# The setup stage of a two-layer diffusion trunk: tiles of x moved ahead of the first modulation's weights

## What is computed

```
silu_c, silu_cc = jax.nn.silu(c), jax.nn.silu(c_ctx)
for l in range(DEPTH):
    mods  = jnp.split((silu_c  @ mod_w[l] + mod_b[l])[:, None, :], 6, axis=-1)
    cmods = jnp.split((silu_cc @ mod_w[l] + mod_b[l])[None, None, :], 6, axis=-1)
    zl = modulate(rmsnorm(xl, norm1_g[l]), mods[0], mods[1])
    zc = modulate(rmsnorm(xc, norm1_g[l]), cmods[0], cmods[1])
    ...
```

## Time and profile before

| | us |
|---|---|
| median of 3 runs (3260.53 to 3262.33) | 3261.51 |
| the profiled execution's own time | 3260.64 |
| its span, first to last instruction | 3258.2 |
| PE busy in the span | 3042.1 (93%) |
| DVE busy | 1581.9 (49%) |
| ACT busy | 1077.6 (33%) |
| mean granted TensorE clock | 0.974 |

### The profile page before, as it was taken

The page is one execution under the profiler, slowest core; times in us unless marked ns, Lnnn a source line. Parts: engine busy times, 40 slices in busy tenths (PEclk is TensorE's granted clock), DMA queues, the critical chain, the costliest instruction groups (busy, mean ns, idle before and its releaser), DMA issues. The chain is left out here.

```text
span 3258.2 us, 40429 instructions
## 1 busy us (share of the span) xinstructions
PE 3042.1 (93%) x17039; PEld 2500.8 (77%) x17039; DVE 1581.9 (49%) x1953; ACT 1077.6 (33%) x1241; POOL 348.5 (11%) x365
## 2 busy tenths in 40 slices
PE   3799895899999999999989999999989999999997
PEld 2577674787888888888877888888867878888886
DVE  3567565336444544444556333333335455445545
ACT  2477575223111111211235434433323222222122
POOL 0011111510000000000023222222110000000002
PEclk8899998999999999999999999999998999999998
DMA  6233331612212211122111111111041111111111
GB/s 255 68 108 106 111 90 35 240 47 91 65 59 65 65 57 54 59 65 65 59 38 39 38 38 39 41 41 40 11 143 46 46 46 46 52 52 46 46 46 52
DMA packets 217451, 220.50 MB, mean 68 GB/s; under 512 B 34366, under 2 KB 191645, under 8 KB 211131
## 3 DMA queue, kind: packets, MB, share of 16 engines
q1 hardware_dynamic: 206443, 161.38, 16.2%
q0 software_dynamic: 10480, 56.52, 5.2%
q10 hardware_dynamic: 352, 0.06, 0.0%
HBM read 191.58 MB, written 26.34 MB: 67 GB/s over the span
## 5 line engine op out<-in xcount | busy, mean ns | idle before, releaser
L741 PE MATMUL ps<-zH,wH 128*128 128x512 f32 (+1 forms) x2160 | 582.3, 369 | 17.4 <-DVE zL L619 11.0
L741 PE MATMUL ps<-zH,wL 128*128 128x512 f32 (+1 forms) x2160 | 578.2, 368 | 0.0
L741 PE MATMUL ps<-zL,wH 128*128 128x512 f32 (+1 forms) x2160 | 578.0, 367 | 0.0
L741 PEld LDWEIGHTS ps<-zH,wH 128*128 128x128 f32 x2160 | 373.7, 188 | 109.0 <-issue 30.3
L741 PEld LDWEIGHTS ps<-zL,wH 128*128 128x128 f32 x2160 | 373.4, 188 | 70.3
L741 PEld LDWEIGHTS ps<-zH,wL 128*128 128x128 f32 x2160 | 373.4, 188 | 70.3
L1824 DVE SCALAR_TENSOR_TENSOR res<-ps,mod,res 128x1024 f32<-128x1024 f32 x240 | 236.7, 1014 | 189.7 <-PE ps L741 178.3
L751 DVE SCALAR_TENSOR_TENSOR V<-ps,vec,V 128x1023 f32<-128x1023 f32 (+1 forms) x132 | 134.1, 1016 | 391.6 <-ACT V L1697 388.5
L1673 ACT ACTIVATE wH<-wraw 128x1024 fp32r<-128x1024 f32 x130 | 134.5, 1050 | 391.9 <-PE ps L741 391.9
L741 PE MATMUL ps<-hH,wH 128*128 128x512 f32 (+1 forms) x700 | 193.2, 373 | 0.0
L741 PE MATMUL ps<-hL,wH 128*128 128x512 f32 (+1 forms) x700 | 191.1, 370 | 0.0
(11 more groups left out here) (276 smaller groups left out, 4627.8 us busy)
## 6 DMA issues: line engine op xcount, KB each, us to landing
wraw<-in_ffn_w_up_dram SPq DMA_DIRECT2D x88, 512.0 KB, 3.8
modw<-in_mod_w_dram POOLq DMA_DIRECT2D x40, 1024.0 KB, 5.3
wraw<-in_ffn_w_down_dram SPq DMA_DIRECT2D x44, 512.0 KB, 3.6
wraw<-in_na_w_in_dram SPq DMA_DIRECT2D x24, 512.0 KB, 4.8
modring<-in_mod_w_dram SPq DMA_DIRECT2D x8, 1024.0 KB, 8.2
wraw<-in_rg_w_in_dram SPq DMA_DIRECT2D x16, 512.0 KB, 6.3
bias<-scratch_bias SPq DMA_DIRECT2D x32, 224.0 KB, 4.2
scratch_yT<-GG POOLq DMA_DIRECT2D x10, 640.0 KB, 3.3
```

The costliest lines, as they stand in the source:

```text
L741: last = nc.tensor.matmul(ps[:, slot * SLOT + c:slot * SLOT + c + n], w(k), r(k)[:, c:c + n], start=(k == 0 and i == 0), stop=(k == K - 1 ...
```

## The change

SP loads x and ctx ahead of all eight blocks of modulation weights; blocks 4 to 7 keep their waits and now follow blocks 0 to 3 directly. PE transposes all eight columns of x directly after the small vectors and runs the eight modulation steps one after the other behind them. A wait of PE for `vec_ready` is dropped; `c_ready`, which it still waits for, comes after it on ACT. The stores of x on SP stand where they stood, behind block 7. ACT's, DVE's and POOL's lists are as before.

```diff
@@ SP @@
             for tile, row, k, s in vec_dmas:
                 sp.dma_start(m.vraw[row:row + k, tile, :], s).then_inc(vec_in, 16)
-            for q in range(4):
-                mod_weights(sp, q)
             for i in range(NT):
                 s = t["x"][0, i * P:(i + 1) * P, :] if i < SEQ // P else t["ctx"][0, i * P - SEQ:(i + 1) * P - SEQ, :]
                 sp.dma_start(m.xraw[:, i, :], s).then_inc(x_in[i], 16)
-            for q in range(4, KD):
-
-                sp.wait_ge(mod_used, q - 3)
+            for q in range(KD):
+                if q >= 4:
+                    sp.wait_ge(mod_used, q - 3)
                 mod_weights(sp, q)
             for f in range(KD):
@@ PE @@
             ins.then_inc(vec_T, 1)
-            pe.wait_ge(c_ready, 2)
-            pe.wait_ge(vec_ready, 2)
-            pe.wait_ge(mod_clear, 1)
-            for k in range(4):
-                modulation(k)
             for f in range(KD):
                 s = f % 2
                 if f >= 2:
@@
                     ins = nc.tensor.transpose(ps[:, s * SLOT + i * P:s * SLOT + i * P + P], m.xraw[:, i, f * P:(f + 1) * P], m.ident[:, :])
                 ins.then_inc(xT_done, 1)
-            for k in range(4, KD):
+            pe.wait_ge(c_ready, 2)
+            pe.wait_ge(mod_clear, 1)
+            for k in range(KD):
                 modulation(k)
             pe.wait_ge(mod_row, 1)
             mod_turn(nc, m).then_inc(mod_T, 1)
```

## The result

The changed kernel takes 3266.39 us, the median of 14 runs (3263.73 to 3273.73), against 3260.39 for the kernel before (14 runs, 3258.76 to 3264.30): **+6.0 us**, a ratio of 1.0020 with a 95% interval of 1.0012 to 1.0028. The interval lies above 1, so the loss is clear of noise; its size lies on the 0.2% line that the prediction drew, and the interval reaches to both sides of it. +6.9 us were forecast. The profiled execution took 3263.73 us and is the fastest of the 14; its span is 3262.0 us against 3258.2. So its stages must be read with care: it shows the mechanism, and less than the usual loss. The 14 runs spread over 10.0 us, those of the kernel before over 5.5.

The account below looks back on a forecast made before the run. DVE was taken to end the setup stage; with the change, block 4's issue at 53.25 plus the drain and 1.15 puts the next stage at 80.0 against 73.15, +6.85 us: 3261.5 + 6.9 = 3268.4 us, range 3264.5 to 3271.0.

Parts of the forecast that it names:

- 0.2% line: 6.5 us, about what a measurement tells from no change; chances: slower by more 0.52, within 0.46, faster by more 0.02.
- What bounds the kernel now: Setup stage: DVE reaches the barrier last, at 72.00 us; modulation had been ready 8.5 us while DVE worked off RG-LRU constants.
- (1): x ahead of the weights on SP: the last of ACT's small loads lands 0.7 us later, at 31.2 us.
- (2): x transposes before steps 0 to 3: first copy at 34.96, last column at 48.97 us, 5.3 us earlier than before.
- (3): SP's wait for step 0, now behind the last column: block 4 issued at 53.25 us instead of 36.17.
- A: The forecast: stores of x land last, last column and step 0 at 1.2 GHz; +6.9 us, chance 0.60.
- B: Rival: PE at 2.4 GHz for the last column's transposes and step 0, 2.0 us less; +4.9 us, chance 0.28.
- (4): Drain of 9.44 MB behind block 4's issue: 4.8 us, then 20.8 us; last store lands at 78.85 us.
- (6): Barrier at the end of setup: next stage starts at 80.0 us against 73.15, +6.85 us; then the same program, shifted.
- (5): Step 7 and DVE's row copy, turn and sums done at 70 to 71 us, hidden some 8 us ahead of the stores.
- Rival C: Block 7 shares the DMA engines with the stores, landing about 78 us, step 7 and DVE following; +10.5 us, chance 0.07.
- D: Rival: stores and loads don't share one limit; stores land at about 71 us, stage ends at 72; -1.3 us, chance 0.05.

Follow-up runs that it names:

- the old order with its weights freed: Kernel before with blocks 4 to 7 in a place of their own and without their waits: 0.9 us below the kernel before, interval across 1.
- one store: Changed kernel storing only column 0 of x, read back for all columns: 1.4 us below the kernel before.
- the repeat: The changed kernel run again unaltered, for a second trace: +5.7 us against the kernel before.
- four stores: Changed kernel without the stores of x columns 4 to 7, columns 0 to 3 read back instead: 0.2 us below the kernel before.
- a busy PE: Changed kernel with eight extra transposes into an unused bank behind each of columns 3 to 6: +3.6 us against the kernel before.
- the last run: Changed kernel without waits for blocks 4 to 7, RG-LRU constants moved between ACT's squares, their DVE addition behind column 4: 3251.07 us.

## Why the prediction was right

*What bounds the kernel now* was right: the old order with its weights freed gains nothing, and the version with the constants moved shows what they cost in the new order.

*(1) Small vectors.* 31.2 was put, 31.27 measured. In the traces with x first they landed at 31.03 to 32.64 (nine of them, in the middle 31.3), with weights first at 30.51, 31.09 and 30.60. The estimate of +0.7 holds for the mean (31.45 against 30.73), but the spread of 1.6 us had been given to the unknown of a single value and not to a difference from run to run. ACT's queue let 72 packets through from 20 to 26 us, between the 50 and 86 of the earlier trace rows.

*(2) The train.* First copy 34.96 forecast, 34.70 measured; last column at 48.97 forecast, 48.27 measured, the 0.5 us put for a late second column being mostly unneeded.

*(3) Block 4's issue* was the mis-sized term in the first trace: 53.25 forecast, 50.95 measured, of which 0.7 came from the train and 1.6 from the clock: the last column took 1.65 us instead of 2.40, and step 0 ran at 2.4 GHz. A and B had been treated as two outcomes of which one would be true. Both are: from the last column's start to the issue it took 4.23 us with PE's order alone and 4.22 with one store, at 1.2 GHz, and 2.34 in the repeat, with four stores and with a busy PE, at 2.4 GHz. The difference, 1.9 us, is what was forecast for it (2.0); its place and price were right, the chances were not (0.60 against 0.28: of six traces with PE's order and the wait, without the extra transposes, two are low there, two high and two between, with 2.68 us in the changed kernel's first trace and 3.86 with six stores moved). So the median of +6.0 lies between A's +6.9 and B's +4.9, and that the sum came within 1 us of it is in part luck.

*(4) and (6) The drain and the barrier.* From block 4's issue to the next stage 4.8 + 20.8 + 1.15 = 26.75 us were forecast; the four traces with all eight stores behind the blocks, at either clock, have 26.9 to 27.0. This is the term that carries the loss, and the experiments with fewer stores check its slope (1.55 us per store measured; 0.655 MB at the 419 GB/s of 66 to 76 us are 1.56). The rate of 419 GB/s from 66 to 76 again is above the about 358 GB/s that the Trainium skill ("DMA: Bandwidth & Descriptors", Specifications) gives as a core's limit.

*(5) The modulation's end* was hidden, as said: DVE's last instruction ended at 68.24 instead of 70 to 71, the earlier issue of block 4 accounting for it. Rival C fell: block 7's step began at 64.37, 12.4 us ahead of the last store's landing. So did D: the share is 1.01 with stores alone, and the last one landed at 76.8 and not about 71. The Trainium skill ("TensorE: Matmul & The Clock Gate", HAM oscillation) advises running all K-tiles ahead of a wait for DMA. The trace agrees for steps 0 to 3, which took 3.61 us in one piece where they took 5.22 before; but three of the steps 4 to 7 ran in 1.88 to 1.89 us each, at the low level, each behind a wait for its block, and the stage ended with the stores all the same.

*The sum* of the profiled execution was 3.8 us too high (3267.5 against 3263.73). 2.2 of it stand at the barrier (80.0 against 77.84), for reasons (2) and (3). 0.8 are the stages behind it (3184.2 against 3185.0), and 0.7 the time outside the span (1.7 us instead of 2.4); neither was forecast. The median's 3268.4 was 2.0 too high, within A's spread; 1.1 of it is the kernel before, at 3260.39 in this group of runs instead of 3261.51. Most signs that were named came a little early with the earlier issue of block 4: its 50.95 against 51 to 54, the stores' issues from 53.90 to 58.4 against 57 to 60, the row's copy at 65.55 against 68, the last landing at 76.8 against 77 to 80. Two slips of the working did no harm: the small loads' -1.1 us is counted from the old 30.5 and is -1.8 from the 31.2 that was taken, so that A spreads over some 4 to 9 us; and the range's lower end, 3264.5 (+3.0), lies below all of B (3.3 to 6.7) and not in its middle part.

As to the sides of the 0.2% line: the measured ratio of 1.0020 with its interval doesn't settle it. What was left out: behind the barrier the rest is not constant. In the twelve traces it takes 3183.1 to 3188.4 us for the same instructions. Part of this stands right at the start. ACT's square root of the sums is queued behind the conversions of two weight tiles, which wait for their DMAs: in the run with six stores moved, from the next stage's first DMA to DVE's first norm instruction it took 17.8 us (71.10 to 88.91), in the kernel before 16.3 (73.15 to 89.43); 1.0 of the 1.5 us stand ahead of the square root, behind the second tile. The forecast said of the first sums that they depend "on the barrier alone". That holds (77.88, 0.04 us behind the first DMA); it does not hold for what follows them, which was put as "the same program, shifted".

## What to carry to other kernels

When instructions are moved up on one engine, look at which queue waits for what is now later, and count all that stands behind that wait: here the first of SP's waits for a step held back 9.4 MB, and the price showed in the drain behind it: 26.9 us from the first issue to the next stage. A gain on the path that ends a stage is kept only if the transfers that it holds back don't end the stage in its place. With room for all eight blocks the same order of PE's work gains 6.7 us instead of losing 6.0, and with six stores moved ahead of the wait the loss is gone. Where a small difference is at stake, one trace is one draw: two traces of this kernel differ by 1.6 us at the same barrier.

## What was not expected of the hardware

- Small DMAs land later beside the weights than beside x, and the time varies: the same 352 packets of ACT's queue were complete at 30.5 to 31.1 us (three traces) when x's 4 KB rows came last, and at 31.0 to 32.6 (nine traces) when the weights' 8 KB rows did. Counted from the end of ACT's last issue the two don't overlap: 4.4 to 4.5 us against 5.0 to 6.0. ACT's issues themselves were 0.5 to 0.7 us later in two traces (last group from 22.19 with PE's order alone and from 22.17 in the repeat, against 21.5 to 21.8 in the others), which is half of the repeat's late landing. That the length of the rows is the reason was not tested by itself.
- The granted clock at one place of a program differs between executions: the last column of x took 1.65 and 1.31 us in the two traces of the changed kernel, and 1.31 or 2.39 to 2.40 in those of kernels whose PE instructions are the same up to there.
- ACT's Square needed no table load of its own after Exp, Ln or Tanh: the squares at 45.48, 51.08 and 53.88 us directly follow them in the last run's trace, with no load between.
